# Turning keys, values and bonus rows of an RWKV-7 scan as 64x64 products into their own rows

## The chip, the cores and the metric

One core of a Trainium2 chip runs the whole kernel in one launch. The metric is device time in microseconds (us), the median of several runs; one more execution was recorded by the hardware profiler, and the views below are of that one. The engines are TensorE (PE; its weight loads are PEld), VectorE (DVE), ScalarE (ACT), GpSimd (POOL) and SyncE (SP). Each works through a queue of its own in order and waits for semaphores that other engines raise.

## What is computed

A two-layer decoder trunk in float32: sequence 512, width 1024. Layer one mixes time by RWKV-7, layer two by differential attention; each is followed by a squared-ReLU MLP of width 4096 and a gated embedding. The change lies in the RWKV-7 recurrence of the first layer, for 16 heads of 64 channels:

```python
def step(S, inp):                      # S: per head, 64 x 64
    r_t, w_t, k_t, v_t, a_t, b_t = inp
    Sa = jnp.einsum('bhvk,bhk->bhv', S, a_t)
    S = S * w_t[:, :, None, :] + Sa[..., None] * b_t[:, :, None, :] + v_t[..., None] * k_t[:, :, None, :]
    y = jnp.einsum('bhvk,bhk->bhv', S, r_t)
    return S, y
_, y = lax.scan(step, S0, (tm(r), tm(w), tm(k), tm(v), tm(a), tm(b)))
```

The output y is then normalised per head, with its mean removed.

## The kernel before

The recurrence is worked out in chunks of 64 positions (CH). A step k of the scan handles one chunk of 8 heads, in four channel tiles of 128 rows, two heads to a tile (QUAD = 4). There are NQ = 16 steps: 0 to 7 carry the first eight heads through the eight chunks, 8 to 15 the others (HALF = 8). The four tiles of a step form two pairs, x = 0 and x = 1, which run half a step apart, so that one pair's products cover the copies of the other.

Inside a step, for each pair, the order is: `state_z` (the state times a, added to what `value_z` left), a copy to Zs, `solve` (times the inverse of the chunk's triangular matrix, TiT), a copy to Us, `answer_y` and `answer_h` (the output and the new state's increment), and the state's decay on VectorE (`state`: Hg, then Hs). The values' parts are `value_z`, `value_y` and `value_h`, from the tiles KV. All of these are 64x64 products: each head has its own half of the rows, and ROWS and SWAP choose the half that the result goes to. The array so holds four independent quarters, and in TensorE's queue products into the same half alternate with products into the other half.

What the change touches prepares these operands. `kv_turn(b)` turns one batch (two tiles, two chunks) of keys and centred values so that position runs along the rows. It writes bank F1. Before, it is two 128x128 transposes with the identity and two 128x128 products with a centring matrix:

```python
for i in range(2):
    pe.transpose(pb[F1][:, 2 * i * P:(2 * i + 1) * P], St[:, K_, c + i, t], ident)
for i in range(2):
    ins = mm(pb[F1][:, (2 * i + 1) * P:(2 * i + 2) * P], St[:, V_, c + i, t], centre[:, :], start=True, stop=True)
```

ScalarE's `kv_taken(b)` empties the bank into KV, in four copies of 64 rows by 256, since what stands together in the bank belongs to other rows and other tiles of KV. The batch b + 1 may be written only when b has been copied. `b_turn(q)` turns the b rows of two chunks in four 128x128 transposes, in every other step, and `b_taken(q)` brings one chunk into NL in two copies (ScalarE for steps below 8, VectorE from 8 on).

`lower_times` and `corner` are products for the next step's inverse; between them stands the copy Xc (`lower_taken`) and after them the copy into TiT (`corner_taken`). `k_score(k + 2)` makes the scores of the step after next, which VectorE masks into KV (`local_scores`) before the bank F2 may be written again. The second half's inverse (`inverse_late`) is spread over VectorE's queue in steps 0 to 7.

The order of everything is written out by hand, one loop over k for each engine. In a matmul of two float32 operands TensorE shows two records per product, in a transpose one.

Of the kernel before, what the change touches and what calls it, by code (L numbers as in the profile page):

```python
# [22 lines left out]
ACT = mybir.ActivationFunctionType  # L23
AX = mybir.AxisListType

P = 128
# [6 lines left out]
HD = 64  # L33
# [107 lines left out]
def trunk(nc, x, p, norm_g, mlp_w1, mlp_w2, ple_w_up, ple_w_gate, rwkv_mix, rwkv_w_rkvo, rwkv_w0, rwkv_w1,  # L141
# [5 lines left out]
    with ctx:  # L147
# [67 lines left out]
        W3 = 3 * CH  # L215
        KV = [at(f"KV{k}", o, [P, QUAD, 4 * CH]) for k, o in enumerate((W_HI, W_LO + 8192, W_HI + 5120, W_LO + 13312))]
        TiT = [at(f"TiT{k}", o, [P, QUAD, CH]) for k, o in enumerate((W_HI + 4096, W_LO + 12288))]
# [123 lines left out]

        def b_rows(q, h):

            n0 = QUAD * (q % HALF)
            return NL[q // HALF][ROWS[h], n0:n0 + QUAD, 0:CH]

        def b_turned(q, h):

            return pb[FB][ROWS[q % 2], :].rearrange("p (u h t) -> p u h t", h=2, t=CH)[:, :, h, :]

# [276 lines left out]
        def _(pe):  # L627
# [185 lines left out]

            def kv_turn(b):

                c, t = batch(b)
                if b:
                    pe.wait_ge(s.kv_ev, b)
                else:
                    pe.wait_ge(s.nl_raw, HALF)  # L820
                    pe.wait_ge(s.dense_a, 36)
                for i in range(2):
                    pe.transpose(pb[F1][:, 2 * i * P:(2 * i + 1) * P], St[:, K_, c + i, t], ident)
                if b == 0:
                    pe.wait_ge(s.cen_in, 16)
                for i in range(2):
                    ins = mm(pb[F1][:, (2 * i + 1) * P:(2 * i + 2) * P], St[:, V_, c + i, t], centre[:, :], start=True, stop=True)
                ins.then_inc(s.kv_mm, 1)

# [13 lines left out]

            def b_turn(q):

                c0 = QUAD * (q // HALF)
                t = slice((q % HALF) * CH, (q % HALF + 2) * CH)
                if q:
                    pe.wait_ge(s.bt_ev, q)
                else:  # L850
# [159 lines left out]
            for q in range(10, NQ):  # L1010
                b_score(q)()
            kv_turn(0)
# [15 lines left out]
            for k in range(NQ):  # L1028
# [439 lines left out]
        def _(act):  # L1468
# [251 lines left out]
            def kv_taken(b):  # L1720

                if b >= NQ:
                    return
                q, x = b // 2 * 2, b % 2
# [342 lines left out]
        def _(dve):  # L2067
# [282 lines left out]
            def b_taken(q):  # L2350

                if HALF <= q < NQ:
                    dve.wait_ge(s.bt_mm, q // 2 + 1)
                    dve.wait_ge(s.x5_mm, q + 1)
                    dve.tensor_copy(b_rows(q, 0), b_turned(q, 0))
                    dve.tensor_copy(b_rows(q, 1), b_turned(q, 1)).then_inc(s.bt_ev, 1)

# [366 lines left out]
```

## Time and profile before

| what | value |
|---|---|
| median of 3 runs | 1449.6 us (1446.9 to 1449.96) |
| the profiled execution | 1448.24 us |
| its span | 1446.0 us |
| TensorE busy | 1381.3 us (96%) |
| VectorE, ScalarE, GpSimd busy | 727.7, 619.3, 549.3 us |
| keys' and values' copies (L1733) | 64, 24.2 us |

The span is what the profiler's rows cover; the execution's own time is 2.2 us longer. A busy TensorE may still be pipelined badly, so a row's start to the next row's start is a better measure of what a block costs than its busy time. A group's line number is the line in the kernel printed above. "Idle before <-releaser" is the time in which an engine had nothing to do before a row, and whose work ended it; "issue" there means that nothing in the profile explains it.

### The profile page before, as it was taken

The numbers are of one execution on the slowest core, as the hardware profiler recorded it, in microseconds if no ns is written. First come the engines' busy times: TensorE is split into PE (matmuls) and PEld (weight loads), VectorE is DVE, ScalarE is ACT, GpSimd is POOL, SyncE is SP. The second block draws the span as 40 slices with busy tenths as digits, with TensorE's granted clock in tenths as the row PEclk, the third lists the DMA queues.
The fourth block names the chain that finished last, engine by engine and source line by source line (L and its number), as shares of the span: only waits on it lengthen the run. The fifth ranks groups of instructions, "written<-read, shape, count | busy, mean of one in ns | idle before, by whom it ended". The sixth has DMA issues, their size and how long they took to land.

```text
span 1446.0 us, 23205 instructions
## 1 busy us (share of the span) xinstructions
PE 1381.3 (96%) x9043; PEld 1154.3 (80%) x9043; DVE 727.7 (50%) x1116; ACT 619.3 (43%) x924; POOL 549.3 (38%) x311
## 2 busy tenths in 40 slices
PE   6999998789999999999999999999999999999998
PEld 5767887675888888888888787766888888888887
DVE  6899987658374300433158453277463301333163
ACT  7885626455433221333254442487433311332262
POOL 3131002214543544344442244345444443445442
PEclk9999999999999999999999999999999999999999
DMA  6212200301223333323233422200232333223231
GB/s 201 82 64 77 70 1 3 125 5 59 87 88 116 104 114 99 102 90 113 91 111 103 147 88 87 87 1 30 76 100 87 116 103 115 87 89 115 95 109 59
DMA packets 119901, 126.44 MB, mean 87 GB/s; under 512 B 6268, under 2 KB 114556, under 8 KB 119816
## 3 DMA queue, kind: packets, MB, share of 16 engines
q1 hardware_dynamic: 119120, 123.99, 26.4%
q8 instruction: 60, 0.98, 0.3%
q0 software_dynamic: 320, 0.66, 0.2%
q10 hardware_dynamic: 376, 0.61, 0.2%
q14 instruction: 25, 0.20, 0.0%
HBM read 123.12 MB, written 2.12 MB: 87 GB/s over the span
## 4 chain that ended last, share of the span: by engine, by line
PE 74%; DVE 12%; ACT 6%; issue 6%; POOL 1%; ACTq 0%; POOLq 0%; DVEq 0%
PE pb L634 21%; PE pb L636 20%; PE pb L635 20%; DVE xl L2476 4%; ACT whi L1485 2%; PE pb L1358 1%; PE pb L764 1%; PE pb L1326 1%; POOL wlo L528 1%; PE pb L1328 1%; PE pb L1327 1%; PE pb L1385 1%; DVE xl L2130 1%; ACT KV L1733 1%; PE pb L1367 1%
## 5 line engine op out<-in xcount | busy, mean ns | idle before, releaser
L525 POOL TENSOR_TENSOR wlo<-wraw,whi 128x1024 fp32r<-128x1024 f32 x96 | 229.9, 2394 | 635.7 <-ACT whi L1485 521.2
L634 PE MATMUL pb<-xh,whi 128*128 128x512 f32 x1088 | 420.0, 386 | 8.1 <-issue 2.6
L635 PE MATMUL pb<-xl,whi 128*128 128x512 f32 x1088 | 413.1, 380 | 0.0
L636 PE MATMUL pb<-xh,wlo 128*128 128x512 f32 x1088 | 413.1, 380 | 0.0
L1485 ACT ACTIVATE whi<-wraw 128x2048 fp32r<-128x2048 f32 x108 | 206.2, 1909 | 261.2 <-PE pb L636 258.1
L634 PEld LDWEIGHTS pb<-xh,whi 128*128 128x128 f32 x1088 | 206.0, 189 | 61.2 <-issue 18.6
L528 POOL TENSOR_TENSOR wlo<-wraw,whi 128x1024 fp32r<-128x1024 f32 x96 | 236.3, 2461 | 0.0
L636 PEld LDWEIGHTS pb<-xh,wlo 128*128 128x128 f32 x1088 | 206.1, 189 | 29.4
L635 PEld LDWEIGHTS pb<-xl,whi 128*128 128x128 f32 x1088 | 206.2, 190 | 28.5 <-issue 1.0
L634 PE MATMUL pb<-hid_h,whi 128*128 128x512 f32 x512 | 194.2, 379 | 0.0
L635 PE MATMUL pb<-hid_l,whi 128*128 128x512 f32 x512 | 194.0, 379 | 0.0
L636 PE MATMUL pb<-hid_h,wlo 128*128 128x512 f32 x512 | 194.0, 379 | 0.0
L2468 DVE TENSOR_TENSOR X<-X,pb 128x512 f32<-128x512 f32 x40 | 25.7, 687 | 249.9 <-PE pb L636 249.9
L1885 ACT ACTIVATE hid_h<-tmp 128x512 fp32r<-128x512 f32 (+1 forms) x64 | 54.6, 899 | 192.2 <-DVE tmp L2506 192.2
L2502 DVE TENSOR_TENSOR tmp<-pb,rstd 128x512 f32<-128x512 f32 x64 | 41.2, 686 | 171.5 <-PE pb L636 171.0
L634 PEld LDWEIGHTS pb<-hid_h,whi 128*128 128x128 f32 x512 | 96.8, 189 | 13.8
L636 PEld LDWEIGHTS pb<-hid_h,wlo 128*128 128x128 f32 x512 | 96.8, 189 | 13.7
L635 PEld LDWEIGHTS pb<-hid_l,whi 128*128 128x128 f32 x512 | 96.8, 189 | 13.7
L2476 DVE SCALAR_TENSOR_TENSOR xl<-X,PV,xh 128x512 fp32r<-128x512 f32 x48 | 65.1, 1418 | 29.2 <-ACT xh L1496 29.2
L2510 DVE TENSOR_TENSOR hid_l<-tmp,hid_h 128x512 f32 x64 | 67.1, 1067 | 17.3 <-ACT hid_h L1885 17.1
L1844 ACT ACTIVATE tmp<-X 128x512 f32<-128x512 f32 x40 | 24.3, 631 | 108.3 <-DVE X L2468 108.3
L2506 DVE SCALAR_TENSOR_TENSOR tmp<-tmp 128x512 f32<-128x512 f32 x64 | 45.7, 756 | 0.0
(324 smaller groups left out, 1795.0 us busy)
## 6 DMA issues: line engine op xcount, KB each, us to landing
wraw<-in_mlp_w_dram SPq DMA_DIRECT2D x128, 512.0 KB, 4.3
wraw<-in_rwkv_w_rkvo_dram SPq DMA_DIRECT2D x32, 512.0 KB, 4.4
wraw<-in_ple_w_gate_dram SPq DMA_DIRECT2D x16, 512.0 KB, 4.3
xtok<-in_x_dram SPq DMA_DIRECT2D x8, 512.0 KB, 6.3
wraw<-in_diff_w_q_dram SPq DMA_DIRECT2D x8, 512.0 KB, 4.0
wraw<-in_w_k_shared_dram SPq DMA_DIRECT2D x8, 512.0 KB, 4.3
wraw<-in_w_v_shared_dram SPq DMA_DIRECT2D x8, 512.0 KB, 4.3
wraw<-in_diff_w_o_dram SPq DMA_DIRECT2D x8, 512.0 KB, 4.0
```

The costliest lines, as they stand in the source:

```text
L525: pool.tensor_tensor(wlo[:, par, front], wraw[:, par, front], whi[:, par, front].bitcast(F32), ALU.subtract)
L528: pool.tensor_tensor(wlo[:, par, rng], wraw[:, par, rng], whi[:, par, rng].bitcast(F32), ALU.subtract).then_inc(s.w_lo, 1)
L634: mm(o, wh, ah, start=first, stop=False)
L635: mm(o, wh, al, start=False, stop=False)
L636: return mm(o, wl, ah, start=False, stop=last)
L1485: A(whi[:, par, :], wraw[:, par, :], ACT.Copy).then_inc(s.w_hi, 1)
L1885: A(hid_h[:, bass.ds(4 * i + 2 * h + m, 1), :].rearrange("p o (a b) -> p o a b", a=2), tmp[:, 2 + m:3 + m, :].rearrange("p o (b a) -> p o ...
L2468: tt(X[:, c, 0:S], X[:, c, 0:S] if old is None else old, b, ALU.add).then_inc(sem, 1)
L2476: stt(lo, x, vec(k, gain), hi, ALU.mult, ALU.subtract).then_inc(s.x_ready, 1)
L2502: tt(tmp[:, m, :], pb[2 * h + m][:, :], rstd[:, :], ALU.mult).then_inc(s.dense_v, 1)
L2506: stt(tmp[:, 2 + m, :], tmp[:, m, :], 0.0, tmp[:, m, :], ALU.max, ALU.mult)\
L2510: tt(hid_l[:, bass.ds(done + m, 1), :].rearrange("p o (a b) -> p o a b", a=2), tmp[:, 2 + m:3 + m, :].rearrange("p o (b a) -> p o a b", a= ...
```

## The change

Keys, values and b rows are turned per head and chunk: each turn is a pair of 64x64 products, one per head, that write straight to the rows, and the place in the bank, from which one copy can bring the whole batch to KV. `kv_turn(b)` becomes eight such pairs, `kv_turn(b, n)`; K uses a 64x64 identity, V a 64x64 block of the centring matrix. `b_turn(q)` becomes eight pairs too. KV is now one tile, KV_two, with the same addresses as before, seen with one more dimension. `kv_taken` is one copy of 128 rows by 512; `b_taken` one of 128 by 256.

The order moves as well. On TensorE the key/value pairs of a step stand between those of `state_z(1)`, `b_turn` and `lower_times`, and `lower_times` comes after `state_z(1)` and, in odd steps, after the turns; it stood ahead of them. On ScalarE `kv_taken(k + 2)` moves from behind `take_y(0, k)` to ahead of `take_u(1, k)`.

```diff
-        KV = [at(f"KV{k}", o, [P, QUAD, 4 * CH]) for k, o in enumerate((W_HI, W_LO + 8192, W_HI + 5120, W_LO + 13312))]
+        KV_two = at("KV_two", W_HI, [P, 2, 6144])
+        KV = [KV_two[:, k % 2, 1280 * (k // 2):1280 * (k // 2) + 1024].rearrange("p (u c) -> p u c", u=QUAD) for k in range(4)]
...
+        def kv_rows(b):
+
+            q, x = b // 2 * 2, b % 2
+            c = 1280 * (q // 2 % 2) + 512 * x
+            return KV_two[:, :, c:c + 512].rearrange("p e (m s t) -> p e m s t", s=2, t=CH)[:, :, :, 1, :]
...
-            def kv_turn(b):
+            def kv_turn(b, n):
...
-                for i in range(2):
-                    pe.transpose(pb[F1][:, 2 * i * P:(2 * i + 1) * P], St[:, K_, c + i, t], ident)
...
-                for i in range(2):
-                    ins = mm(pb[F1][:, (2 * i + 1) * P:(2 * i + 2) * P], St[:, V_, c + i, t], centre[:, :], start=True, stop=True)
-                ins.then_inc(s.kv_mm, 1)
+                e, i, value = n // 4, n // 2 % 2, n % 2
+                w = slice(t.start + e * CH, t.start + (e + 1) * CH)
+                for h in range(2):
+                    turn = centre[ROWS[h], h * HD:(h + 1) * HD] if value else unit(h)
+                    ins = mm(pb[F1][SWAP[h], n * CH:(n + 1) * CH], St[ROWS[h], V_ if value else K_, c + i, w], turn,
+                             start=True, stop=True)
+                if n == 7:
+                    ins.then_inc(s.kv_mm, 1)
...
-                for u in range(QUAD):
-                    ins = pe.transpose(pb[FB][:, u * P:(u + 1) * P], St[:, A_, c0 + u, t], ident)
-                ins.then_inc(s.bt_mm, 1)
+                e, u = n // 4, n % 4
+                w = slice((q % HALF + e) * CH, (q % HALF + e + 1) * CH)
+                for h in range(2):
+                    ins = mm(pb[FB][ROWS[h], n * CH:(n + 1) * CH], St[ROWS[h], A_, c0 + u, w], unit(h), start=True, stop=True)
+                if n == 7:
+                    ins.then_inc(s.bt_mm, 1)
...
-            b_turn(0)
-            kv_turn(1)
+            for n in range(8):
+                b_turn(0, n)
+                kv_turn(1, n)
...
-                if inner:
-                    for u in range(QUAD):
+                for i in range(2):
+                    state_z(1, k, i)
+                    if ahead:
+                        kv_turn(k + 2, i)
+                if inner and k % 2:
+                    for n in range(8):
+                        b_turn(k + 1, n)
+                        if ahead and n < 6:
+                            kv_turn(k + 2, n + 2)
+                for u in range(QUAD):
+                    if inner:
                         lower_times(k + 1, u)
-                state_z(1, k, 0)
-                state_z(1, k, 1)
-                if inner and k % 2:
-                    b_turn(k + 1)
-                if ahead:
-                    kv_turn(k + 2)
+                    if ahead and k % 2 == 0:
+                        kv_turn(k + 2, u + 2)
+                if ahead and k % 2 == 0:
+                    kv_turn(k + 2, 6)
+                    kv_turn(k + 2, 7)
...
-                turned = pb[F1][:, :].rearrange("p (i j h t) -> p i j h t", i=2, j=2, t=CH)
-                for e in range(2):
-                    kv = KV[(q + e) % 4][:, 2 * x:2 * x + 2, :].rearrange("p i (b t) -> p i b t", t=CH)
-                    for h in range(2):
-                        ins = A(kv[SWAP[h], :, 1:4:2, :], turned[ROWS[e], :, :, h, :], ACT.Copy)
-                ins.then_inc(s.kv_ev, 1)
+                A(kv_rows(b), pb[F1][:, :].rearrange("p (e m t) -> p e m t", e=2, t=CH), ACT.Copy).then_inc(s.kv_ev, 1)
...
-                    A(b_rows(q, 0), b_turned(q, 0), ACT.Copy)
-                    A(b_rows(q, 1), b_turned(q, 1), ACT.Copy).then_inc(s.bt_ev, 1)
+                    A(b_rows(q), b_turned(q), ACT.Copy).then_inc(s.bt_ev, 1)
...
                 b_taken(k + 1)
+                kv_taken(k + 2)
                 take_u(1, k)
                 take_y(0, k)
-                kv_taken(k + 2)
```

TensorE in step 11, an odd one, from the solve of pair 0 to the first answers (pb6 takes keys and values, pb4 the b rows). Before:

```order
L977 MATMUL pb0<-Zs0_98,TiT1_84 64x64 x2
L913 MATMUL pb1<-KV3_82 64x64 x2
L977 MATMUL pb0<-Zs0_98,TiT1_84 64x64 x2
L867 MATMUL pb5<-inv_d1_89,NL1_94 64x32 x8
L953 MATMUL pb1<-Hs1_97,St_70 64x64 x4
L853 MATMUL pb4<-cst_67,St_70 128x128 x4
L823 MATMUL pb6<-cst_67,St_70 128x128 x2
L827 MATMUL pb6<-centre_76,St_70 128x128 x2
L991 MATMUL pb2<-NL1_94,Us0_100 64x64 x2
```

Now, from the same solve; the last two rows below go on in the same way until eight pairs of each kind are done, and then `lower_times` follows:

```order
L988 MATMUL pb0<-Zs0_95,TiT1_81 64x64 x2
L924 MATMUL pb1<-KV_two_79 64x64 x2
L988 MATMUL pb0<-Zs0_95,TiT1_81 64x64 x2
L964 MATMUL pb1<-Hs1_94,St_70 64x64 x2
L834 MATMUL pb6<-cst_67,St_70 64x64 x2
L964 MATMUL pb1<-Hs1_94,St_70 64x64 x2
L834 MATMUL pb6<-centre_76,St_70 64x64 x2
L863 MATMUL pb4<-cst_67,St_70 64x64 x2
L834 MATMUL pb6<-cst_67,St_70 64x64 x2
L863 MATMUL pb4<-cst_67,St_70 64x64 x2
L834 MATMUL pb6<-centre_76,St_70 64x64 x2
L863 MATMUL pb4<-cst_67,St_70 64x64 x2
```

The turns stood in one block behind `lower_times` (L867); now they alternate pair by pair, begin within `state_z` (L964), and `lower_times` is behind them.

ScalarE in a step of the first half, from the copy Zs of pair 1 on (L1742, L1743 and now L1758 are the b rows, L1733 and now L1750 the keys and values). Before:

```order
L1769 ACTIVATE Zs1_99<-pb1 128x128
L1742 ACTIVATE NL0_93<-pb4 64x4x64
L1743 ACTIVATE NL0_93<-pb4 64x4x64
L1775 ACTIVATE Us1_101<-pb1 128x128
L1782 ACTIVATE St_70<-pb2 128x2x64
L1733 ACTIVATE KV0_79<-pb6 64x4x64 x2
L1733 ACTIVATE KV1_80<-pb6 64x4x64 x2
L1759 ACTIVATE TiT0_83<-pb5 128x4x32
L1769 ACTIVATE Zs0_98<-pb0 128x128
```

Now:

```order
L1784 ACTIVATE Zs1_96<-pb1 128x128
L1758 ACTIVATE NL0_90<-pb4 128x4x64
L1750 ACTIVATE KV_two_79<-pb6 128x2x4x64
L1790 ACTIVATE Us1_98<-pb1 128x128
L1797 ACTIVATE St_70<-pb2 128x2x64
L1774 ACTIVATE TiT0_80<-pb5 128x4x32
L1784 ACTIVATE Zs0_95<-pb0 128x128
L1790 ACTIVATE Us0_97<-pb0 128x128
L1797 ACTIVATE St_70<-pb3 128x2x64
```

Four copies behind the second Us and St have become one ahead of them.

## Rows read from the trace of the kernel before

**Rows 1.** Windows: span, then busy us (instructions) of each engine; granted clock; DMA share.
```profile
222.00:229.00 7.00, 6.00 (x130) 5.46 (x124) 5.49 (x6) 2.98 (x11) 0.07 (x1) 0.76 0.01 2
...
229.00:251.00 22.00, 18.76 (x652) 17.02 (x652) 18.50 (x51) 14.83 (x50) 7.38 (x12) 1.00 0.02 4
...
277.00:284.00 7.00, 4.18 (x151) 3.77 (x155) 2.38 (x6) 2.85 (x10) 1.57 (x3) 1.00 0.99 363
...
297.00:303.00 6.00, 5.65 (x196) 5.21 (x198) 3.48 (x10) 3.17 (x12) 1.82 (x5) 1.00 0.01 3
```

**Rows 2.** Groups by line and shape, ScalarE, whole span: count, busy us, mean ns.
```profile
L1733 ACT ACTIVATE KV<-pb 64x256 f32<-64x256 f32 x64 | 24.2, 379 | 2.1 <-PE pb L827 1.2
...
L1650 ACT ACTIVATE NL<-pb 128x512 f32<-128x512 f32 x16 | 9.2, 597 | 4.7 <-PE pb L764 4.7
```

**Rows 3.** Timeline, scan's start: start us, us, engine, line, operation [idle before <-releaser].
```profile
219.57 1.55 ACT L1733 ACTIVATE KV<-pb 64x256 f32<-64x256 f32 x4 [0.97 <-PE pb L827]
...
221.56 0.48 PE L882 MATMUL pb<-inv_dt,Xc 64*64 64x32 f32 x10 [0.92 <-ACT Xc L1751]
...
222.97 0.69 DVE L2331 TENSOR_TENSOR KV<-pb,cst 128x512 f32<-128x512 f32 x1 [3.07 <-PE pb L839]
...
226.80 1.25 DVE L2288 STREAM_TRANSPOSE inv_d<-inv_t 128x1024 f32<-128x1024 f32 x1
```

**Rows 4.** Timeline, VectorE and TensorE, steps 4 and 5.
```profile
253.95 0.29 DVE L2370 TENSOR_TENSOR Hg<-pb,Hs 128x128 f32<-128x128 f32 x1 [0.53 <-PE pb L1001]
...
257.57 0.29 DVE L2372 TENSOR_TENSOR Hs<-Hg,small 128x128 f32<-128x128 f32 x1
...
258.01 0.45 PE L953 MATMUL pb<-Hs,St 64*64 64x64 f32 x8
```

**Rows 5.** Timeline, TensorE, step 11 and the solve of step 12.
```profile
299.23 0.61 PE L867 MATMUL pb<-inv_d,NL 64*64 64x32 f32 x16
299.67 0.43 PE L953 MATMUL pb<-Hs,St 64*64 64x64 f32 x8
300.02 0.66 PE L853 MATMUL pb<-cst,St 128*128 128x128 f32 x4
300.52 0.38 PE L823 MATMUL pb<-cst,St 128*128 128x128 f32 x2
300.73 0.61 PE L827 MATMUL pb<-centre,St 128*128 128x128 f32 x4
301.27 0.27 PE L991 MATMUL pb<-NL,Us 64*64 64x64 f32 x2
...
301.80 0.23 PE L913 MATMUL pb<-KV 64*64 64x64 f32 x2
...
302.10 0.43 PE L966 MATMUL pb<-St,Hs 64*64 64x64 f32 x8
302.36 0.26 PE L882 MATMUL pb<-inv_dt,Xc 64*64 64x32 f32 x4
...
304.71 0.27 PE L977 MATMUL pb<-Zs,TiT 64*64 64x64 f32 x2
```

**Rows 6.** Timeline, ScalarE, end of step 11.
```profile
302.34 0.28 ACT L1775 ACTIVATE Us<-pb 128x128 f32<-128x128 f32 x1 [1.92 <-PE pb L977]
...
302.81 1.55 ACT L1733 ACTIVATE KV<-pb 64x256 f32<-64x256 f32 x4
304.38 0.28 ACT L1769 ACTIVATE Zs<-pb 128x128 f32<-128x128 f32 x1
```

**Rows 7.** Timeline, VectorE, step 11.
```profile
299.88 0.35 DVE L2340 TENSOR_SCALAR Xc<-pb,cst 128x128 f32<-128x128 f32 x1 [0.74 <-PE pb L867]
...
302.54 0.68 DVE L2331 TENSOR_TENSOR KV<-pb,cst 128x512 f32<-128x512 f32 x1
```

**Rows 8.** Timeline, TensorE, step 9.
```profile
283.66 0.33 PE L839 MATMUL pb<-St 64*64 64x128 f32 x2 [2.33 <-issue]
...
290.32 0.21 PE L977 MATMUL pb<-Zs,TiT 64*64 64x64 f32 x1 [2.74 <-issue]
```

More of the change, by code:

```diff
@@ L340, in batch, with b_rows, b_turned @@
             return QUAD * (q // HALF) + 2 * (b % 2), slice((q % HALF) * CH, (q % HALF + 2) * CH)
-        def b_rows(q, h):
+        def b_rows(q):
             n0 = QUAD * (q % HALF)
-            return NL[q // HALF][ROWS[h], n0:n0 + QUAD, 0:CH]
-        def b_turned(q, h):
-            return pb[FB][ROWS[q % 2], :].rearrange("p (u h t) -> p u h t", h=2, t=CH)[:, :, h, :]
+            return NL[q // HALF][:, n0:n0 + QUAD, 0:CH]
+        def kv_rows(b):
+            q, x = b // 2 * 2, b % 2
+            c = 1280 * (q // 2 % 2) + 512 * x
+            return KV_two[:, :, c:c + 512].rearrange("p e (m s t) -> p e m s t", s=2, t=CH)[:, :, :, 1, :]
+        def b_turned(q):
+            return pb[FB][:, (q % 2) * 256:(q % 2 + 1) * 256].rearrange("p (u t) -> p u t", t=CH)
         def head_tile(i):
@@ L812, in unit @@
                 return ident[ROWS[h], ROWS[h]]
-            def kv_turn(b):
+            def kv_turn(b, n):
                 c, t = batch(b)
-                if b:
+                if n == 0 and b:
                     pe.wait_ge(s.kv_ev, b)
-                else:
+                elif n == 0:
                     pe.wait_ge(s.nl_raw, HALF)
                     pe.wait_ge(s.dense_a, 36)
-                for i in range(2):
-                    pe.transpose(pb[F1][:, 2 * i * P:(2 * i + 1) * P], St[:, K_, c + i, t], ident)
-                if b == 0:
                     pe.wait_ge(s.cen_in, 16)
-                for i in range(2):
-                    ins = mm(pb[F1][:, (2 * i + 1) * P:(2 * i + 2) * P], St[:, V_, c + i, t], centre[:, :], start=True, stop=True)
-                ins.then_inc(s.kv_mm, 1)
+                e, i, value = n // 4, n // 2 % 2, n % 2
[6 more added lines that the diff above has]
+                    ins.then_inc(s.kv_mm, 1)
             def k_score(q, u):
@@ L842, in k_score, with b_turn @@
                     ins.then_inc(s.ks_mm, 1)
-            def b_turn(q):
+            def b_turn(q, n):
                 c0 = QUAD * (q // HALF)
-                t = slice((q % HALF) * CH, (q % HALF + 2) * CH)
-                if q:
+                if n == 0 and q:
                     pe.wait_ge(s.bt_ev, q)
-                else:
+                elif n == 0:
                     pe.wait_ge(s.nl_raw, NQ)
-                for u in range(QUAD):
-                    ins = pe.transpose(pb[FB][:, u * P:(u + 1) * P], St[:, A_, c0 + u, t], ident)
-                ins.then_inc(s.bt_mm, 1)
+                e, u = n // 4, n % 4
[4 more added lines that the diff above has]
+                    ins.then_inc(s.bt_mm, 1)
             def lower_times(q, u):
@@ L1011, in _ @@
                 b_score(q)()
-            kv_turn(0)
+            for n in range(8):
+                kv_turn(0, n)
             for u in range(QUAD):
                 k_score(0, u)
-            b_turn(0)
-            kv_turn(1)
+            for n in range(8):
+                b_turn(0, n)
+                kv_turn(1, n)
             for u in range(QUAD):
@@ L1051, in _ @@
                 solve(0, k, 1)
-                if inner:
-                    for u in range(QUAD):
-                        lower_times(k + 1, u)
-                state_z(1, k, 0)
-                state_z(1, k, 1)
-                if inner and k % 2:
-                    b_turn(k + 1)
-                if ahead:
-                    kv_turn(k + 2)
+                for i in range(2):
[3 more added lines that the diff above has]
+                if inner and k % 2:
+                    for n in range(8):
+                        b_turn(k + 1, n)
[3 more added lines that the diff above has]
+                    if inner:
+                        lower_times(k + 1, u)
+                    if ahead and k % 2 == 0:
[3 more added lines that the diff above has]
+                    kv_turn(k + 2, 7)
                 answer_y(0, k, 0)
@@ L1723, in kv_taken @@
                     return
-                q, x = b // 2 * 2, b % 2
+                q = b // 2 * 2
                 act.wait_ge(s.kv_mm, b + 1)
@@ L2354, in b_taken @@
                     dve.wait_ge(s.x5_mm, q + 1)
-                    dve.tensor_copy(b_rows(q, 0), b_turned(q, 0))
-                    dve.tensor_copy(b_rows(q, 1), b_turned(q, 1)).then_inc(s.bt_ev, 1)
+                    dve.tensor_copy(b_rows(q), b_turned(q)).then_inc(s.bt_ev, 1)
             def state(x, k):
```

## Prediction

> **What bounds the kernel now.** I read the windows first. The change touches only the scan, from 216 to 325 us of the span; what stands before and after it is the same program, and what follows waits for the scan's end, so the scan's saving is the kernel's. TensorE has work in most of that time [rows 1], but not the same thing bounds each stretch.
>
> *The start, 216 to 229 us.* ScalarE empties the second batch of turned keys and values in four copies, 1.55 us from 219.57; only then comes its copy Xc, for which TensorE's corner products wait 0.92 us; behind them stand the scores that VectorE awaits for 3.07 us [rows 3]. VectorE then has four block pieces in a row, the last from 226.80 to 228.05. From 222 to 229 us the granted clock averages 0.76 [rows 1].
>
> *Steps 1 to 6, to 272 us.* A loop through VectorE closes each step: it starts with Hg(0) when TensorE's answers of pair 0 are there (idle 0.53 us before 253.95), does the scores' mask and four inverse operations, and ends with Hs(1) at 257.86; TensorE's state_z(1) starts just then [rows 4]. VectorE is busy 18.50 of 22 us here [rows 1]. A saving elsewhere counts only if it lies between state_z(1) and the answers.
>
> *Steps 7 to 15.* VectorE has no inverse left (3.48 of 6 us busy) and TensorE's own queue is the bound [rows 1]. One odd step [rows 5]: lower_times 0.44 us (299.23 to 299.67), state_z(1) 0.35, four turns for b 0.50, two for the keys 0.21, two value products 0.54, then 32 records of answers in 0.53. ScalarE holds it up once per step: between Us at 302.34 and Zs at 304.38 stand the four copies, 1.55 us, and TensorE's solve(0), next in its queue at about 304.4, starts at 304.71 [rows 6].
>
> **What a new product costs.** The trace has no 64x64 product with an identity, but has 64x64 products in plenty. The 32 records of the answers (two per product; two products into their own rows, two into the swapped rows, at once) take 0.53 us, so one product takes 0.13 us in its quarter of the array, whether the other quarters work or not: eight records of state_y, which have only two quarters busy, take 0.26 us, which is 0.13 for each pair [rows 5]. The bounds: below, 0.11, as the four pairs of lower_times take 0.44; above, 0.27, if a product cost what a full-size value product does (two in 0.54), which is the world of rival D. I take 0.12 to 0.13, because shape, type and neighbours are those of the answers.
>
> **The change, part by part, on TensorE.** Odd step: state_z(1) with two of eight key/value pairs beside it 0.25 (it was 0.35 because a 128x128 turn followed it), eight b pairs with the other six beside them 1.0, lower_times 0.44: 1.7 us against 0.44 + 0.35 + 0.50 + 0.75 = 2.04, saving **0.35**. Even step (no b): state_z with two 0.25, lower_times with four 0.5, two pairs alone 0.25: 1.0 against 0.44 + 0.35 + 0.75 = 1.54, saving **0.55**. The six or eight key/value pairs beside others are costed at nothing; the cover is the diagonal products in the other quarters, and without it they are 0.13 each.
>
> **On ScalarE.** Four copies of 379 ns become one of 128x512, for which L1650 shows 597 ns [rows 2]; 1.55 becomes 0.60. It also moves in front of take_u(1). There ScalarE idles 1.92 us up to 302.34 in the second half [rows 6], so the copy fits as soon as its products are done, and Zs(0) no longer waits: **0.3** in each step that TensorE bounds, nothing where VectorE does. The two b copies become one, on ScalarE in the first half and VectorE in the second; I cost that at nothing, since it stands in idle time of both, and if it did not, it would be a gain.
>
> **What lower_times behind the turns costs.** Xc and the b copy wait for it. In the second half both stand on VectorE ahead of state(0) and of the scores' mask. In an odd step, counted from the start of state_z(1), Xc starts at about 2.0 us instead of 0.21 (299.88), so the mask starts at 3.35 instead of 2.87 (302.54) and ends at 4.0 [rows 7]. TensorE's next score product wants its bank at about 3.8. That is a new wait of 0.2 to 0.3 us in steps 9 and 11; step 13 has no score product left to wait. State_z(1) also loses its cover: it now follows the solve directly, and Hs(1) may be 0.1 late.
>
> **Sum.** Start: the second batch is copied 0.6 instead of 1.55 after a turn that itself starts 1.0 earlier (its bank frees earlier) but takes 0.4 longer; Xc comes 1.1 earlier, and the answers of step 0 another 0.3: **-1.4**. Steps 1 to 6: the leg from state_z(1) to the answers is 1.1 (0.35 + 0.75) before and 1.0 now in even steps, 1.6 and 1.7 in odd ones less what the last record's end gives back: **-0.3**. Steps 7 and 8: **-0.8** (0.2 and 0.6). Steps 9 and 11: -0.35 - 0.3 + 0.3 + 0.1, about -0.2 each; 13: -0.5; 10 and 12: -0.55 - 0.3 + 0.05 = -0.8 each: **-2.5**. Steps 14 and 15 have no turns: 0. Together -5.0. The profiled execution took 1448.24 us, so it would take 1443.2; the median of the three runs, 1449.6, is 1.4 above it, which gives 1444.6. The four executions scatter by 3 us, and I forecast **1444**, between the two. The rivals' times below start from the median. No difference under 0.2% (2.9 us) can be told from none here, so the forecast is just beyond that.
>
> **Rivals.**
> *A: the clock stays up (15%).* TensorE waits 0.92 us before 221.56 and soon again for the scores' mask; after that the granted clock averages 0.76, part of it at the lower level of 1.2 GHz [rows 1, 3]. With the first gap gone it may stay at 2.4 GHz; step 0's products (about 4 us at 1.2 GHz) then end up to 1.5 us earlier, of which VectorE's pieces let little more than 1 through. With the lower product bound: 1442.
> *B: the gain is eaten on the way (24%).* The turns give 768 matmul records instead of 128 (256 and 128 products of two records each against 16 times 6 and 8 times 4), in a scan of about 2900 (652 in 22 us), so code must be fetched 20% more often. While loads arrive (queues 0.99 busy from 277 to 284 us) TensorE stood 2.33 and 2.74 us with nothing to wait for [rows 1, 8]. A third such stop costs 2.5 us and leaves -2.5: 1447. The same result comes if the start saves nothing because VectorE's pieces decide.
> *C: slower through ScalarE's order (5%).* In the first half lower_taken stands before take_z(1), and now waits for the later lower_times; behind it come the b copy and the 0.6 us copy, then take_u(1). In an odd step I get Us(1) at 3.5 us after state_z(1), some 0.8 later than now, and TensorE reaches the next state_z(1) at 5.9, where Hs(1) comes at 6.6. So 0.7 us of slack is left. From there on it decides. If it costs 2.0 us more per step than I count, steps 1 to 6 add 1.3 us each, 7.8 in all; less the 4.7 saved elsewhere, the time is 1453.
> *D: the quarters do not share (4%).* Key/value and b pairs use the same row halves of the array. So do the 32 records of the answers, which overlap fully [rows 5]. If these did not, eight pairs in odd steps and six in even ones would add 0.13 each: 14 batches, 12.7 us, less the 5.0: 1457. The Trainium skill, "TensorE: Matmul & The Clock Gate", Part 3, says that a weight load overlaps running matmuls only when the row group differs, which would speak for D. With that rule the trace does not agree: 32 records in four quarters are 0.066 us for each of a quarter's eight, the 0.065 of state_y, where only two quarters work.
> That the change does not do what it says is excluded by the order of instructions above: the copies and products are there as described.
>
> **Numbers.** Forecast 52%, A 15%, B 24%, C 5%, D 4%. Faster by over 0.2%: forecast and A, 67%. Within: B, 24%. Slower: C and D, 9%. The range for eight in ten holds forecast, A and B with the product's bounds: 1440 (A with everything 2 us better) to 1448.5 (B with another 1.5 lost); C and D are left out, and the tails.
>
> **What would show it.** The copy L1750 at 0.6 us, once per batch, and Zs(0) within 0.4 us of state_z(0) in steps 9 to 14; even steps of the second half near 4.8 us from state_z(1) to state_z(1) and odd ones near 5.5 (both 5.5 to 5.8 now); the first half still paced by Hs(1); score products that wait for VectorE's mask in steps 10 and 12; two stops of some 2.5 us around 280 to 290. It is wrong if the turn blocks take more than 1.2 us, if ScalarE's Us(1) sets the step in the first half, or if a third stop appears.

## The result, and the profile after

| | before | changed |
|---|---|---|
| median | 1446.9 us (1444.45 to 1449.96, 13 runs) | 1455.25 us (1453.07 to 1458.9, 13 runs) |
| ratio of changed to before | | 1.006, 95% interval 1.0051 to 1.0069 |
| span of the profiled run | 1446.0 us | 1452.9 us |

The change makes the kernel 8.4 us slower. The forecast was 1444.0, faster; the result lies outside the range of 1440 to 1448.5.

The page of the changed kernel, its head, the engines' busy times and the queue through which instructions are fetched:

```profile
span 1452.9 us, 24421 instructions
...
PE 1373.1 (95%) x9683; PEld 1150.5 (79%) x9683; DVE 723.3 (50%) x1108; ACT 598.6 (41%) x868; POOL 548.4 (38%) x311
...
q8 instruction: 65, 1.06, 0.3%
```

Before, the same lines were:

```profile
span 1446.0 us, 23205 instructions
...
q8 instruction: 60, 0.98, 0.3%
```

TensorE's busy time went down (1381.3 before) and ScalarE's too (619.3), and yet the program is longer. What went up is the number of instructions: by 1216, which is 640 matmuls and 640 weight loads more and 64 copies less. The instruction queue brought five packets of 16 KB more, one for each 243 added instructions.

The copies came out as described (groups by line and shape: count, busy us, mean ns); they answer to the first line of [rows 2]:

```profile
L1750 ACT ACTIVATE KV_two<-pb 128x512 f32<-128x512 f32 x16 | 9.6, 602 | 10.1 <-PE pb L834 10.1
...
L1758 ACT ACTIVATE NL<-pb 128x256 f32<-128x256 f32 x8 | 3.1, 385 | 0.0
```

Windows of the changed kernel, the same four stretches as [rows 1] (span, then busy us and instructions of PE, PEld, DVE, ACT, POOL; granted clock; DMA share):

```profile
222.00:229.00 7.00, 4.76 (x204) 4.66 (x208) 6.10 (x8) 2.51 (x9) 1.57 (x3) 0.94 0.01 2
229.00:251.00 22.00, 17.42 (x702) 16.07 (x698) 17.57 (x48) 8.02 (x30) 5.30 (x9) 0.86 0.02 4
277.00:284.00 7.00, 4.85 (x206) 4.26 (x196) 2.97 (x8) 2.27 (x9) 3.14 (x6) 1.00 0.54 189
297.00:303.00 6.00, 4.48 (x208) 3.98 (x201) 2.74 (x8) 2.04 (x7) 1.57 (x3) 1.00 0.03 7
```

From 297 to 303 us TensorE ran 208 matmuls where it had run 196, but was busy 4.48 instead of 5.65 us, and VectorE and ScalarE are idle for longer too. Nobody is the bound in that row. In the first half the granted clock, 1.00 before, now averages 0.86.

The chain of waits from 300 to 325 us says who is (its line of shares, which the view cuts off; then pieces: start, us, what):

```profile
by line: issue 29.5%; PE pb L964 7.5%; PE pb L863 6.9%; PE pb L936 6.0%; PE pb L1002 5.7%; PE pb L893 4.5%; PE pb L834 4.5%; PE pb L1012 4.5%; PE pb L977 4.2%; PE pb L988 4.1%; PE pb L878 4.0%; PE pb L848 3.8%; PE pb L947 3.7%; ACT St L1797
...
302.83 0.77 issue
...
306.60 1.50 issue
...
311.05 1.09 issue
...
314.76 1.21 issue
```

"Issue" is time in which TensorE waited for nothing that the profile shows. It is 29.5% of the chain here. In the matching stretch of the kernel before, 297 to 320 us, it is 10.7%, and the key and value copies, which the change was to shorten, are 11.1%:

```profile
by line: ACT KV L1733 11.1%; issue 10.7%; PE pb L977 9.2%; PE pb L867 7.7%; PE pb L953 6.8%; PE pb L1001 6.8%; PE pb L913 6.5%; PE pb L991 6.3%; PE pb L827 5.8%; PE pb L853 5.1%; PE pb L925 4.9%; ACT St L1782 4.2%; PE pb L839 3.6%; PE pb L8
```

So the copies did leave the path. Something else took more than their place. The chain's pieces belong to these rows of TensorE's timeline (start, us, engine, line, operation, idle before and its releaser), one view for each row's surroundings:

```profile
308.10 0.21 PE L1002 MATMUL pb<-NL,Us 64*64 64x64 f32 x1 [1.50 <-issue]
```

```profile
312.14 0.27 PE L977 MATMUL pb<-St,Hs 64*64 64x64 f32 x2 [1.09 <-issue]
```

```profile
315.96 0.27 PE L988 MATMUL pb<-Zs,TiT 64*64 64x64 f32 x3 [1.21 <-issue]
```

Such stops, 0.48 to 1.50 us long, stand at 299.74, 303.60, 308.10, 312.14, 315.96, 319.88, 323.83 and 328.10 us, at six different lines of the program. Counting what lies between two stops explains them. Windows cut at the stops:

```profile
299.74:303.60 3.86, 2.87 (x125) 2.62 (x124) 1.48 (x4) 1.32 (x4) 1.57 (x3) 1.00 0.02 4
303.60:308.10 4.50, 2.82 (x126) 2.61 (x125) 1.26 (x4) 1.32 (x4) 0.00 (x0) 1.00 0.01 4
308.10:312.14 4.04, 2.70 (x125) 2.50 (x125) 2.06 (x6) 0.72 (x3) 1.57 (x3) 1.00 0.02 4
312.14:315.96 3.82, 2.56 (x124) 2.29 (x124) 1.84 (x5) 1.32 (x4) 0.00 (x0) 1.00 0.02 4
315.96:319.88 3.92, 2.92 (x126) 2.57 (x126) 0.88 (x3) 1.44 (x6) 1.57 (x3) 1.00 0.02 4
```

Each holds 124 to 126 matmuls and 124 to 126 weight loads, 248 to 252 records, whatever the work is; TensorE is busy for 2.6 to 2.9 us with them and then stands. The seven intervals up to 328.10 us take 28.36 us, 4.05 each. The instruction queue moves one packet of 16 KB in each of them (at 301.3, 305.5, 309.5, 313.5 and 317.2 us). TensorE has used up a block of instructions and stands until the next is there. In the kernel before, packets come at the same pace (299.3, 303.2, 307.3, 311.2, 315.2 us), 4.0 apart, and from 297 to 321 us TensorE ran 782 matmuls and as many loads, 65 records per us, against 871 of each in the 28.36 us of the changed kernel, 61 per us. It stood only 0.15 to 0.35 us now and then. Even before, this stretch of the scan used nearly all the instructions that could be brought; the profile did not show it, because the blocks were just in time.

The start of pair 1's state product in each step (state_z(1), us of the span) shows where the time goes:

| step | before | changed | difference |
|---|---|---|---|
| 1 | 232.04 | 229.96 | -2.1 |
| 3 | 245.28 | 244.61 | -0.7 |
| 5 | 258.01 | 259.50 | +1.5 |
| 7 | 271.88 | 273.90 | +2.0 |
| 9 | 284.99 | 288.21 | +3.2 |
| 11 | 299.67 | 304.67 | +5.0 |
| 13 | 311.12 | 318.92 | +7.8 |
| 15 | 322.15 | 332.32 | +10.2 |

Behind the scan some 3 of the 10.2 us are regained (the spans differ by 6.9); where was not looked into. How far two traces of one program differ can be seen in e1 below, which turned out to be the kernel before once more: its state_z(1) starts 0.3 us later in step 1, 0.4 in step 7, 1.6 in step 9 and 0.5 in step 15.

### The profile page after: what moved, and what is told of

It is laid out like the page before. It is cut to its first block, busy times and chain, and to the rows that moved or that the text cites. A ratio compares the mean times of both kernels' runs of the same rounds, so it can differ in the third digit from the quotient of the medians.

```text
span 1452.9 us, 24421 instructions
## 1 busy us (share of the span) xinstructions
PE 1373.1 (95%) x9683; PEld 1150.5 (79%) x9683; DVE 723.3 (50%) x1108; ACT 598.6 (41%) x868; POOL 548.4 (38%) x311
## 4 chain that ended last, share of the span: by engine, by line
PE 73%; DVE 12%; issue 7%; ACT 6%; POOL 1%; ACTq 0%; DVEq 0%; POOLq 0%
PE pb L641 20%; PE pb L643 20%; PE pb L642 20%; DVE xl L2490 3%; ACT whi L1506 2%; PE pb L1379 1%; PE pb L1347 1%; PE pb L771 1%; POOL wlo L535 1%; PE pb L1349 1%; PE pb L1348 1%; PE pb L1406 1%; PE pb L1388 1%; DVE xl L2145 1%; DVE X L2482 1%
```

## The experiments

Theories. **S, supply:** TensorE's instructions come in blocks of some 250 records, one per 4.05 us on average, so each added record costs 16 ns where TensorE already takes them as fast as they come, even if the product itself runs in a free quarter of the array. **O, order:** the loss comes from `lower_times` behind the turns, which delays Xc, the inverse and the masks. **W, work:** the small products themselves cost more array time than counted.

Eleven versions were run (twelve runs). Ratios are to the kernel before, run beside each on the same chip: its median was 1446.79 us beside e1 to e4, 1447.62 beside e5 to e9, 1445.85 beside e10 to e12 and 1446.67 beside e13. The ratio is estimated from all runs, so it can differ from the quotient of two medians by 0.0005.

| run | instructions more | median us | ratio (95%) |
|---|---|---|---|
| the change | 1216 | 1455.25 | 1.006 (1.0051 to 1.0069) |
| e1_nops | 0 | 1447.57 | 0.9998 (0.9984 to 1.0011) |
| e2_kv_only | 784 | 1455.26 | 1.0069 (1.0048 to 1.009) |
| e3_b_only | 432 | 1452.48 | 1.0045 (1.0029 to 1.0062) |
| e4_lower_first | 1216 | 1454.55 | 1.0056 (1.0035 to 1.0076) |
| e5_many_small | 896 | 1460.08 | 1.0085 (1.0061 to 1.0109) |
| e8_few_long | 224 | 1450.70 | 1.0027 (1.0015 to 1.0039) |
| e9_pairs_left_out | 600 | 1449.17 | 1.0018 (1.0005 to 1.0031) |
| e7_copies_split | 0 | 1448.95 | 1.0011 (1.0 to 1.0022) |
| e10_start_only | 152 | 1445.44 | 1.0002 (0.9988 to 1.0015) |
| e11_first_half | 657 | 1448.49 | 1.0016 (1.0001 to 1.0031) |
| e12_second_half | 559 | 1453.75 | 1.0054 (1.0034 to 1.0074) |
| e13_start_again | 152 | 1445.92 | 0.9998 (0.9987 to 1.0009) |

### e1_nops: instructions without work

```diff
+                for _ in range(80):
+                    pe.nop()
```

> The kernel before with 80 no-operation instructions of TensorE added at the head of each of the 16 steps: 1280 in all, about as many as the change adds (640 matmul records and 640 weight loads). No product, copy, wait or order is changed. Theory S (TensorE's code arrives in blocks at a bounded rate, one per about 4 us in steps 9 to 14 of the changed kernel, and the change's extra instructions run into that bound): 8 to 14 us slower than before, with new stops of 0.5 to 2.5 us marked issue in steps 1 to 15, five more packets of the instruction queue. Theory O (the new order leaves TensorE idle for VectorE, so its clock falls, and that costs the time): no slower than the no-operations' own time, which is 80 x 16 times the few ns that the trace shows for one, no new stops and a clock as before.

Measured: nothing, because nothing was added. The compiled program has the same 23205 instructions and 60 packets as before; the no-operations are not in it. It is a repeat of the kernel before (ratio 0.9998) and says nothing about S.

### e2_kv_only and e3_b_only: each half of the change alone

e2, key and value turns and copy new, b turns as before (against the changed kernel; in odd steps four of the eight key/value pairs then stand beside `lower_times` and two alone):

```diff
                 if inner and k % 2:
-                    for n in range(8):
-                        b_turn(k + 1, n)
-                        if ahead and n < 6:
-                            kv_turn(k + 2, n + 2)
+                    b_turn(k + 1)
...
```

> Keys and values as 64x64 products with one copy per batch, as in the changed kernel; the b rows as four 128x128 transposes with two copies, as before. Adds 832 of the 1280 instructions. Theory S: between the two kernels, nearer the changed one: 1450 to 1453 us where before is 1447 and changed 1455. Theory O: as slow as the changed kernel, since state_z(1) stands ahead of lower_times here too: 1454 to 1456.

e3, the other way round (against the kernel before, whose order stays):

```diff
                 if inner and k % 2:
-                    b_turn(k + 1)
+                    for n in range(8):
+                        b_turn(k + 1, n)
                 if ahead:
                     kv_turn(k + 2)
```

> The b rows as eight pairs of 64x64 products with one copy; keys and values in two transposes, two products and four copies, and the order of the kernel before. Adds 448 of the 1280 instructions, and 0.4 to 0.5 us of TensorE work in each of seven odd steps. Theory S: +3 to +5 us over before (work and code together). Theory O: +1 to +3, from the work alone, and no new stops.

Measured: 1.0069 and 1.0045. Both halves lose, and they do not add up to the whole (1.006): the halves' losses are 10.0 and 6.5 us by their intervals' centres, against 8.7. e2 has the single key and value copy and two thirds of the added instructions and is no faster than the whole, so the b turns alone are not the culprit. Its 1455.26 us is what O had expected (1454 to 1456) and not what S had (1450 to 1453). e3, in the old order, lost a little more than S gave it (3 to 5 us) and much more than O did (1 to 3). The two theories stand one against one here; e4 is the run that separates them.

Part of what makes e2 so dear is in its trace. From 216 to 330 us TensorE waits for ScalarE's copies far longer than in the changed kernel (total us, times, longest). In e2:

```profile
PE pb L934 <- ACT St L1793: 8.8, 14, 2.0
...
PE pb L922 <- ACT KV_two L1745: 1.9, 1, 1.9
```

In the changed kernel:

```profile
PE pb L936 <- ACT St L1797: 4.5, 10, 2.0
```

The single copy L1745 holds TensorE up once, for 1.9 us before 241.46 us. The stops marked issue add up to less in e2 than in the changed kernel (about 10 us against 18).

### e4_lower_first: the changed kernel with lower_times ahead again

```diff
+                for u in range(QUAD):
+                    if inner:
+                        lower_times(k + 1, u)
+                    if ahead:
+                        kv_turn(k + 2, u)
                 for i in range(2):
                     state_z(1, k, i)
...
```

> The changed kernel with lower_times ahead of state_z(1) again, as in the kernel before; the key/value pairs stand between its products and those of state_z(1) and b. Same instructions, another order. Theory O: most of the loss comes back: within 2 us of before, the clock above 0.95 from 229 to 272 us. Theory S: 1 to 3 us better than the changed kernel at most, the stops marked issue in steps 9 to 15 as long as there (about 18 us over the scan).

Measured: 1454.55, ratio 1.0056, inside the change's own interval. Order has an effect, but a local one: steps 1 to 7 take 41.6 us instead of 43.9 (39.8 before), and the granted clock of 229 to 251 us is 1.00 again (0.96 from 229 to 272 us, as O had it). But the time does not come back. Stops about one block apart stand here already from 240.40 us on, and from step 7 to 15 it takes 60.6 us against 58.4 of the changed kernel. O falls as the main cause; what it gives, the next late block eats.

The same trace shows that the pace is not TensorE's own. Before the first of these stops it ran 230 matmuls and 230 weight loads in 4.00 us without a pause, 115 records per us:

```profile
226.48:230.48 4.00, 4.00 (x230) 3.99 (x230) 3.19 (x13) 1.93 (x8) 0.00 (x0) 1.00 0.02 4
```

### e5_many_small and e8_few_long: products added to the kernel before

e5 puts eight pairs of 16-column products into each of 14 steps, e8 two pairs of 256 columns. Both write a bank that is free at that moment, their results are not used, and no copy waits for them; TensorE waits for the bank (`kv_ev`) earlier than before.

```diff
+            def pad(n):
+                for h in range(2):
+                    mm(pb[F1][SWAP[h], 0:n], St[ROWS[h], K_, 0, 0:CH], St[ROWS[h], K_, 1, 0:n], start=True, stop=True)
...
+                if ahead:
+                    pe.wait_ge(s.kv_ev, k + 2)
...
+                    if ahead:
+                        pad(16)                  # e8: pad(256), at two of the eight places
```

> The kernel before with eight pairs of idle 64x64 products of 16 columns per step (steps 0 to 13), in the swapped quarters beside lower_times and state_z(1); they write the key bank before the turns overwrite it. 64 more instructions per step, 896 in all, in quarters that have nothing to do, and at most 0.2 us of TensorE time of their own. Theory S (bounded supply of TensorE's code): +5 to +9 us over before, stops marked issue between steps 1 and 14, four more packets of the instruction queue. Theory O or any theory of order and waits: +0 to +2.

> The control of the run with many small products: two pairs of 256 columns per step instead of eight of 16, in the same quarters, banks and places, so as much or more array time, and 16 instructions per step instead of 64 (224 in all). Theory S: +0 to +3 us over before. A theory of quarters that disturb each other: as slow as the many small ones or slower.

Measured: 12.5 us for 896 records, 3.1 us for 224 (medians). Per added record that is 14 ns in both, and 14 ns for the 672 by which they differ, but the intervals are wide: 9 to 16 us for e5, 2 to 6 us for e8. e8's products move four times as many columns in all (per step 4 of 256 against 16 of 16) and cost a quarter, so it is not the columns that cost. How much of e8's 3.1 us is its own products or the earlier wait for the bank was not separated: it has no more stops marked issue than the kernel before, and TensorE's waits for the copies Zs and St are longer (6.1 us in all against 4.7). S at 16 ns gives 14.6 and 3.6 us. My expectation for e5 was too low.

e5 also has four times as many weight loads as e8, so the two runs alone don't tell the supply of instructions from the loads' own time. The pace does. Windows from one packet of the instruction queue to another, in the kernel before (five packets), the changed kernel (six) and e5 (seven):

```profile
299.29:319.53 20.24, 18.91 (x642) 17.04 (x640) 11.53 (x32) 10.05 (x35) 3.63 (x7) 1.00 0.02 3
...
301.27:325.34 24.07, 16.48 (x752) 15.10 (x753) 9.05 (x27) 6.65 (x24) 5.18 (x10) 1.00 0.02 3
...
297.44:326.22 28.78, 24.98 (x891) 22.69 (x893) 13.55 (x38) 11.85 (x40) 6.34 (x12) 0.92 0.02 4
```

That is 4.05, 4.01 and 4.11 us for each packet, while TensorE is busy for 93%, 68% and 87% of the time. The time of a block doesn't follow the work in it, which excludes W in this stretch.

The trace of e5 also shows that a late block is worse under load (timeline row and window between this stop and the next one):

```profile
289.49 0.36 PE L925 MATMUL pb<-KV 64*64 64x64 f32 x1 [2.85 <-issue]
```

```profile
289.49:295.54 6.05, 4.23 (x124) 4.12 (x125) 0.93 (x3) 1.00 (x4) 0.00 (x0) 0.50 0.70 248
316.81:324.89 8.08, 6.48 (x249) 5.93 (x250) 3.62 (x10) 3.24 (x11) 1.59 (x3) 1.00 0.02 4
```

249 records took 6.05 us while the DMA queues were 0.70 busy, and 4.04 each when they were not (499 records in 8.08 us). In the first of these rows the granted clock was 0.50, the lower level, after the stop of 2.85 us.

### e9_pairs_left_out: fewer of the hidden pairs

The changed kernel without most of the key and value pairs (two or three of eight are left in each batch from the third on; copies, waits and order stay). It leaves out that part of the computation, the turned keys and values of those positions.

```diff
             def kv_turn(b, n):
...
+                if b >= 2 and (0 < n < 6 or (n == 6 and b % 2)):
+                    return
```

> The changed kernel without those key/value pairs (in batches 2 to 15) that stand beside other products: five of eight in even steps, six in odd ones, 616 instructions in all. The bank's old content is copied in their place, so this part of the computation is left out; all copies, waits, b turns and the order stay. Theory S: 6 to 10 us faster than the changed kernel, near the kernel before. Theory O (order and waits): within 1.5 us of the changed kernel, as the pairs took no time of their own.

Measured: 1449.17 against 1455.25, so 616 records that the prediction costed at nothing cost 6.1 us (the same by the two ratios, 1.006 and 1.0018), 10 ns each. Its page:

```profile
span 1446.3 us, 23805 instructions
...
q8 instruction: 62, 1.02, 0.3%
```

Three packets fewer than the changed kernel. With 600 instructions more than before it still loses 0.18%.

### e7_copies_split: the kernel before, copies in two parts

```diff
+                if k >= 6:
+                    kv_taken(k + 2, (0,))
                 take_u(1, k)
                 take_y(0, k)
-                kv_taken(k + 2)
+                kv_taken(k + 2, (1,) if k >= 6 else (0, 1))
```

> The kernel before with the four copies of keys and values split from step 6 on: two ahead of take_u(1), two where all four stood. No product or order of TensorE changes. If ScalarE's copies cost TensorE its 0.3 us per step in the second half, as the prediction had it: 1 to 2.5 us faster than before. If TensorE's code supply bounds those steps: within 0.7 us of before.

Measured: 1448.95, ratio 1.0011. No instruction is added, and two of the four copies leave the way of Zs(0). The scan's step 15 starts at 321.55 instead of 322.15 us in its trace, which is no more than two traces of one kernel differ, and the timed runs show no gain: the medians are 1.3 us apart the other way, more than the 0.7 that S allowed, with an interval that begins at none. So even the 0.3 us per step that the prediction gave to the copies cannot be found in the times. That where the blocks come just in time a shorter wait for ScalarE ends in a longer one for the next block would explain it, but was not tested.

### e10, e11, e12, e13: the change by stretch

One kernel with both forms, and a condition that says which steps use the new one (order, turns and copies of that step alike):

```diff
+        def new_step(k):
+            return k < 0          # e10, e13; e11: k < 7; e12: k >= 7
...
+                if not new_step(k):
+                    if inner:
+                        for u in range(QUAD):
+                            lower_times(k + 1, u)
+                    state_z(1, k, 0)
+                    state_z(1, k, 1)
```

> The new turns and the single copies for batches 0 and 1 and for the first b turn only; every later step as before (TensorE: 160 instructions more than before instead of 1216 net). If the supply of TensorE's instructions is what ate the gain (S), the start keeps its saving, since only half a 16 KB block more is fetched: state_z(1) of step 1 about 2 us earlier than before, still 1.5 to 2 us earlier in step 7, and the time 1445.5 to 1446.5 against 1447.6 of before. If the start's saving is absorbed by VectorE's block pieces or by the next fetch stop (rival), step 7 stands where it stood and the time is 1447 to 1448.

> The whole change for steps up to 6 (batches 0 to 8, b turns of the first eight chunks), the rest as before: 692 instructions more. S: the first half turns a lead of 2 us into a lag of about 2 by step 7, as in the changed kernel, and the second half keeps it: 1449 to 1450.5. If all of the loss comes from the second half (rival: only there is TensorE the bound), 1446 to 1447.

> The whole change for steps from 7 on (batches 9 to 15, b turns of the second eight chunks), the start and the first half as before: 588 instructions more. S: TensorE there is already fed no faster than it works, so 5 to 6 us are lost: 1452 to 1454, with a stop every 4 us from about 297 us of the span on. If what costs is a lead that the changed first half has lost, and not the second half's own instructions (rival), 1447 to 1449.

> The start-only version once more, to narrow its interval. If the 2.5 us by which its scan ends earlier in its profile reach the end of the kernel, the median is 0.1 to 0.2% below before's; if the later stages take the lead back (rival), the ratio is 1.000 again.

Measured: start only 1.0002 and 0.9998, start and first half 1.0016, second half 1.0054. The starts of state_z(1), as differences to the kernel before:

| step | e10 start | e11 first half | e12 second half | the change |
|---|---|---|---|---|
| 1 | -2.5 | -2.5 | +0.5 | -2.1 |
| 7 | -2.2 | +1.1 | +0.9 | +2.0 |
| 15 | -2.5 | +1.2 | +6.0 | +10.2 |

The start keeps its lead of 2.5 us to step 15, as S said, with 152 instructions more (in e13's trace the lead is 1.8 in step 1 and 1.9 in step 15). The first half turns -2.5 into +1.1. The second half loses 5.1 us between steps 7 and 15 of its trace, and 7.9 us in the medians, more than the 5 to 6 expected (the profiled execution, 1450.76 us, was the fastest of its six, 3.0 below their median). It adds 588 records; at 16 ns that is 9.4 us, less the 3.3 that the prediction's own sum gives these steps leaves 6.1. The windows between its stops have the signature again:

```profile
299.80:307.57 7.77, 5.49 (x249) 5.00 (x250) 2.95 (x9) 2.09 (x7) 1.67 (x3) 1.00 0.02 4
307.57:311.53 3.96, 2.74 (x125) 2.46 (x124) 1.27 (x4) 1.60 (x5) 0.00 (x0) 1.00 0.02 4
311.53:315.33 3.80, 2.81 (x126) 2.56 (x126) 2.06 (x6) 0.72 (x3) 1.59 (x3) 1.00 0.02 4
```

e10 and e13 do not beat the kernel before by what can be measured: their profiled spans are 3.5 and 2.6 us shorter, but their medians stand 0.4 and 0.8 us below those of the kernel before, within the intervals. The spans flatter them: the execution profiled before took 1448.24 us, 1.3 above that kernel's median. A lead of 1.8 to 2.5 us is there in the scan of each trace, but all of 2.5 us (a ratio of 0.9983) lies outside both intervals; where it is lost was not settled. Of the versions that keep a part of the change and compute the whole reference, e10 (with e13, its repeat) is the only one for which no cost can be measured.

## Why the prediction was wrong

**Windows and bound.** For steps 7 to 15 the prediction said that "TensorE's own queue is the bound". That was half of it. TensorE was busy 5.65 of 6 us [rows 1], but at 65 records per us it was also at the pace at which its instructions arrive. Neither fact can be read from the other; the second needs the count of records per us, which [rows 1] holds, and the times of the packets of the instruction queue, which I did not look at.

**What a new product costs.** Right for the array. The b and key/value pairs share it as the answers do. Timeline of the changed kernel, step 5, from state_z(1) to `lower_times`:

```profile
259.50 0.27 PE L964 MATMUL pb<-Hs,St 64*64 64x64 f32 x2 [0.68 <-DVE Hs L2386]
259.52 0.27 PE L834 MATMUL pb<-cst,St 64*64 64x64 f32 x2
...
259.79 0.23 PE L863 MATMUL pb<-cst,St 64*64 64x64 f32 x2
...
260.49 0.40 PE L863 MATMUL pb<-cst,St 64*64 64x64 f32 x8
260.72 0.55 PE L878 MATMUL pb<-inv_d,NL 64*64 64x32 f32 x14
```

Between 259.79 and 260.72 us lie the 32 matmul records of eight b pairs and most of the key and value pairs, 0.93 us where 1.0 was expected. Rival D is out. The rule that the prediction had quoted for it, of the Trainium skill, "TensorE: Matmul & The Clock Gate", Part 3, is that a weight load overlaps running matmuls only when the row group differs; these pairs share their row halves with others and still took 0.93 us.

**"The six or eight key/value pairs beside others are costed at nothing."** This is the step that failed. The array has room for them; the supply of instructions has not. e9 gives their price: 6.1 us for 616 records. From the 5.0 us that the sum saved to the 8.4 that were lost it is 13.4 us; the other 7.3 lie with the remaining 664 added records, which the sum costed by their time in the array alone (at 10 to 16 ns each, the prices of e9 and S, an estimate of 7 to 11 us), and with the order.

**Rival B** had the mechanism and the wrong size. It named the code that "must be fetched 20% more often" and then charged it with one more stop of 2.5 us, as if only stops under load counted. The stops under load did get no more numerous (2.89 at 285.62 and 2.40 at 292.04 us, against 2.33 and 2.74 in [rows 8]). What came instead is a stop at each block, 0.5 to 1.5 us, also when the DMA queues are 0.02 busy. It also counted matmuls alone, 640; the weight loads are as many, so the added records are 1280, and at 16 ns they are 20 us where nothing else hides them.

**Odd and even steps, -2.5 in all.** The array's saving may be there, but cannot be seen under the stops: between steps 9 and 15 the changed kernel takes 44.1 us, the kernel before 37.2, instead of 2.5 less. Step 11, which was to take 5.5 us, takes 8.2, and step 12, which was to take 4.8, takes 6.0.

**ScalarE.** The copy took 0.60, as said, and in the chain of the changed kernel no copy L1750 is among the first dozen lines. The 0.3 us per step behind it did not materialise (e7). Rival C's mechanism, ScalarE's order, was not seen in the changed kernel: TensorE never waits for Us in its scan. In e2 the waits for St and for the single copy come near to it.

**Start, -1.4.** Right in sign, and larger: -2.1 in the changed kernel, -2.5 in e10. Rival A's first half was right too, the granted clock of 222 to 229 us rose from 0.76 to 0.94, and to 1.00 in e10. But the gain was lost by step 5.

**Steps 1 to 6, -0.3.** Wrong: +3.6 us in e11 between steps 1 and 7. Two things lie in it that the runs separate in part. With `lower_times` ahead again (e4) steps 1 to 7 are 2.4 us shorter than in the changed kernel at the same instruction count, and the clock stays at 1.00 up to 251 us; so about 2.4 us are order and the lower clock, which comes with longer waits (2.03 us before 227.35, 1.94 before 237.99 us). The rest, 1.7 us of e4 against before, fits supply, as e4 has stops marked issue here, but no run shows it by itself. How the 2.4 divide between the late inverse and the lower clock stays open.

**What stays open** besides that: why e2 loses as much as the whole change. Its 784 instructions at 16 ns are 12.5 us, less about 2.5 at the start and 3 in the steps is 7; measured were 10.0 with an interval of 6.9 to 13.0. Its longer waits for ScalarE's copies, and a granted clock of 0.72 to 0.91 in its windows from 251 to 310 us (0.74 to 0.98 in the changed kernel), might be the rest; no run tests it.

## What to carry to other kernels

Before many small instructions take the place of a few large ones, count the records per us that the engine already executes in that stretch and compare them with the pace of its instruction packets: here about 250 records per 4 us, 61 to 65 per us, is the ceiling over several blocks, and work that is hidden in a free quarter of the array still cost 10 ns (e9) to 14 ns (e5) per record there. The sign of it in a trace is a stop with no releaser after each equal number of records, at ever other lines. A stretch in which another engine sets the pace can hide some of it, but not twice the instructions.

## What the runs showed of the hardware

The supply of TensorE's instructions is the finding that I had not expected: one block of about 250 records per 4 us (3.82 to 4.50 between neighbouring stops from 299.74 us on, 4.05 on average, in the changed kernel; 4.04 in e5; 3.80 to 3.96 in e12), with DMA queues nearly idle (0.02). The packet itself takes a part of it: it is seen 1.1 to 1.9 us after TensorE went on (309.5 after 308.10, 313.5 after 312.14, 317.2 after 315.96), lasts 0.9 to 1.5 us, and TensorE goes on again 2.3 to 2.8 us after its start.

The Trainium skill, "Runtime: NRT & Kernel Launch", section "Instruction fetch mechanics", says that code is refilled in blocks of 256 instructions, the next while the current one runs, that TensorE's store holds 2048 instructions, and that the fetch is hidden because the sequencer dispatches more slowly than the store is filled. The trace agrees with the size of the block (about 250 records and a few waits between stops). It does not agree that the fetch is hidden: TensorE was through each block after 2.6 to 3.4 us (308.10 to 311.05, 312.14 to 314.76, 315.96 to 319.40) and stood for the rest of 4.05. Nor does any run show a reserve of several blocks: the burst of 460 records in 4.00 us in e4 is less than two.

Under load the same block is later: 6.05 us between two stops at a DMA share of 0.70 in e5.

A late block can cost twice. After the stop of 2.85 us in e5 the granted clock was at the lower level, 1.2 GHz (0.50 from 289.49 to 295.54 us), and around the stops of 2.89 and 2.40 us of the changed kernel it averages 0.74 from 284 to 296 us. In the kernel before it stayed at 1.00 in those 12 us in spite of stops of 2.33 us, just before them, and 2.74; what decides between the two was not tried.
